# A hybrid DeltaNet, retention and ConvFFN layer: two whole-tile FFN pairs instead of three, and weight splits moved at the v tiles

## What is computed

```python
def mixer_block(hn, pos, w_in, conv_w, a_log, dt_bias, gdn_norm, w_out):
    proj = hn @ w_in                      # q, k, v, z, decay, rotary q and k, retention v, gates
    qkv = silu(causal_dwconv(concat([gq, gk, gv]), conv_w))
    o_a = gated_delta_chunked(gq, gk, gv, log_g, beta)
    o_b = retention_chunked(rq, rk, rv)
    y = sigmoid(gate_a) * y_a + sigmoid(gate_b) * y_b
    return y @ w_out

def conv_ffn(hn, w_up, conv_w, conv_b, w_down):
    u = causal_dwconv(hn @ w_up, conv_w) + conv_b
    a, b = split(u, 2, axis=-1)
    return (silu(a) * b) @ w_down
```

## Time and profile before

| what | before |
|---|---|
| median of 3 runs | 1952.65 us (1951.92 to 1953.54) |
| the profiled execution | 1952.48 us |
| its span, first to last instruction | 1950.7 us |
| PE busy | 1927.2 us, 99% of the span |
| DVE busy | 1283.2 us, 66% |
| ACT busy | 796.1 us, 41% |
| POOL busy | 332.2 us, 17% |
| PE instructions | 13173 matmuls, each with a weight load |

### The profile page before, as it was taken

How to read it: one execution, slowest core, us unless ns; L and a number is a source line. 1 busy time by engine, 2 the same in 40 slices (tenths; PEclk the granted TensorE clock), 3 DMA queues, 4 the chain that set the end, 5 groups by cost and what they waited for, 6 DMA issues and landing times.

```text
span 1950.7 us, 32138 instructions
## 1 busy us (share of the span) xinstructions
PE 1927.2 (99%) x13173; PEld 1859.5 (95%) x13173; DVE 1283.2 (66%) x1612; ACT 796.1 (41%) x1094; POOL 332.2 (17%) x327
## 2 busy tenths in 40 slices
PE   8999999999999999999999999999999999999998
PEld 7999997999999999999999999999999999988887
DVE  6456764747675767677544334389988889877656
ACT  5223432534343444444443333234444344445443
POOL 0000002566574122221101101200000000000001
PEclk9999999999999999999999999999999999999999
DMA  9666566655555575555545552222433555578654
GB/s 296 222 205 141 129 169 191 201 173 161 166 185 141 145 212 162 172 144 157 162 114 157 169 147 87 87 90 60 130 100 109 152 152 162 152 263 277 192 189 159
DMA packets 301222, 315.99 MB, mean 162 GB/s; under 512 B 151004, under 2 KB 221124, under 8 KB 300948
## 3 DMA queue, kind: packets, MB, share of 16 engines
q1 hardware_dynamic: 291860, 290.86, 48.1%
q0 software_dynamic: 9216, 23.07, 5.9%
HBM read 222.76 MB, written 114.18 MB: 173 GB/s over the span
## 4 chain that ended last, share of the span: by engine, by line
PE 92%; DVE 3%; DMA 2%; ACT 1%; issue 1%; POOL 1%; DVEq 0%; SPq 0%; ACTq 0%; POOLq 0%
PE a_psum L1171 35%; PE a_psum L1467 18%; PE a_psum L1477 11%; PE a_psum L155 11%; PE a_psum L1158 5%; PE a_psum L1258 1%; PE a_psum L1277 1%; DMA w_raw<-in_w_in 1%; PE a_psum L1255 1%; PE a_psum L1363 1%; PE a_psum L1287 1%; PE a_psum L1347 1%; PE a_psum L1378 1%; PE a_psum L1303 1%; PE a_psum L1386 1%
## 5 line engine op out<-in xcount | busy, mean ns | idle before, releaser
L1171 PE MATMUL a_psum<-xh,w_hi 128*128 128x342 f32 (+3 forms) x1632 | 528.7, 324 | 3.0 <-DVE w_lo L1936 1.9
L1171 PE MATMUL a_psum<-xl,w_hi 128*128 128x342 f32 (+3 forms) x1632 | 523.1, 321 | 0.0
L1171 PE MATMUL a_psum<-xh,w_lo 128*128 128x342 f32 (+3 forms) x1632 | 521.3, 319 | 0.0
L1171 PEld LDWEIGHTS a_psum<-xh,w_hi 128*128 128x128 f32 x1632 | 307.2, 188 | 6.1 <-DVE w_lo L1936 2.5
L1171 PEld LDWEIGHTS a_psum<-xl,w_hi 128*128 128x128 f32 x1632 | 307.3, 188 | 0.8
L1171 PEld LDWEIGHTS a_psum<-xh,w_lo 128*128 128x128 f32 x1632 | 307.1, 188 | 0.0
L1622 ACT ACTIVATE post<-a_psum 128x342 f32<-128x342 f32 (+3 forms) x204 | 93.2, 457 | 486.0 <-PE a_psum L1171 455.0
L1936 DVE TENSOR_TENSOR w_lo<-w_raw,w_hi 128x1024 fp32r<-128x1024 f32 x86 | 111.1, 1292 | 131.4 <-ACT w_hi L1547 131.3
L1547 ACT ACTIVATE w_hi<-w_raw 128x1024 fp32r<-128x1024 f32 x86 | 90.6, 1053 | 100.8 <-PE a_psum L155 63.0
L1467 PE MATMUL a_psum<-x_t_hi,up_hi 128*128 128x256 f32 x608 | 123.6, 285 | 2.7 <-DVE post L2424 2.5
L1477 PE MATMUL a_psum<-act_hi,down_hi 128*128 128x512 f32 (+1 forms) x324 | 124.4, 384 | 0.0
(11 more groups left out here) (294 smaller groups left out, 3954.9 us busy)
## 6 DMA issues: line engine op xcount, KB each, us to landing
w_raw<-in_w_in SPq DMA_DIRECT2D x75, 512.0 KB, 3.8
up_raw<-in_w_up SPq DMA_DIRECT2D x19, 1024.0 KB, 5.0
mix_scratch<-post SPq DMA_DIRECT2D x32, 522.0 KB, 2.8
down_sums<-in_w_ffn_down POOLq DMA_DIRECT2D x4, 2816.0 KB, 29.4
act_scratch<-post SPq DMA_DIRECT2D x22, 512.0 KB, 2.7
down_raw<-down_sums SPq DMA_DIRECT2D x44, 256.0 KB, 2.7
act_raw<-act_sums SPq DMA_DIRECT2D x44, 256.0 KB, 3.0
ext<-mix_scratch SPq DMA_DIRECT2D x9, 1024.0 KB, 7.6
```

The costliest lines, as they stand in the source:

```text
L1171: mm = pe.matmul(psum[:, u % 2, 0:n], w[:, k, :], x[:, k, at0:at0 + n], start=(k == 0 and part == 0), stop=(k == KC - 1 and part == 2))
```

## The change

`J0` goes from 3 to 2: pair 2 becomes the first Strassen pair, and everything that stood at `J0 - 1` and `J0 - 2` moves one pair earlier. A semaphore `x_free` is incremented by PE when the last whole tile has read blocks 0 to 3 of `xh` and `xl`; the high parts 1 and 3 and the sum `x_t4` wait for it and no longer for the whole tile. DVE's order in between is rewritten. The semaphore that this takes is won by folding `pe_xss` into `rms_ready`.

In `front_plan()`, at the last two v tiles: `dec` and `dec_e` of chunk 0 move from step 91 to step 92, which is behind ACT's copy of third (46, 2); the load of tile 48 moves in front of the stores of tile 44's turned v; and the split of tile 48 moves from behind third (47, 0) to step 92, in front of the turning of v tile 45. (Step u is the third (16 + u // 3, u % 3).)

```diff
-J0 = 3
+J0 = 2
...
-        if j == 0 and not T_RV - 1 <= t < T_Q - 1:
+        if j == 0 and not T_RV - 1 <= t < T_Q - 1 and t != T_ZB - 1:
             add(("split", t + 1))
...
-    steps[91] += [("dl_k", 0), ("expand", 0), ("dec", 0), ("dec_e", 0)]
-    steps[92] += [("qk", 0), ("dl_g", 1), ("dl_m", 1), ("dl_x", 1)]
+    steps[91] += [("dl_k", 0), ("expand", 0)]
+    steps[92] += [("dec", 0), ("dec_e", 0), ("qk", 0), ("dl_g", 1), ("dl_m", 1), ("dl_x", 1)]
...
-        if u == 93:
+        if u in (90, 93):
             weights(t, j)
             add(("vstore", t - 2))
         for step in sorted(steps[u], key=lambda step: step[0] in ("tin", "tout")):
             add(step)
-        if u == 95:
-            add(("split", T_ZB + 1))
+        if u in (92, 95):
+            add(("split", T_ZB + u // 95))
...
-            if u != 92:
+            if u not in (89, 92):
                 add(("vstore" if T_V <= t - 1 else "kstore", t - 1))
-        if t > T_K and u != 93:
+        if t > T_K and u not in (90, 93):
             weights(t, j)
...
                 if ks[-1] == KC - 1:
                     mm.then_inc(units_done, 3)
+                elif t == T_UP + 2 * J0 - 1:
+                    mm.then_inc(x_free, 1)
...
-                    up(j, s, range(KC))
+                    up(j, s, range(KC // 2))
+                    up(j, s, range(KC // 2, KC))
...
             def x_part_high(n):
-                if n not in (0, 2):
+                if n in (1, 3):
+                    act.wait_ge(x_free, 1)
+                elif n > 3:
                     act.wait_ge(units_done, tiles_done(T_UP + 2 * J0 - 1))
...
-                    dve.wait_ge(units_done, tiles_done(T_UP + 2 * J0 - 1))
+                    dve.wait_ge(x_free, 1)
                     dve.wait_ge(x_prep, x_sum_of(1))
...
                 if j == J0 - 1:
                     taps(j, 0)
                     x_part_low(2)
+                    x_part_low(3)
                 evacuate(j, 1)
...
-            x_part_low(3)
             x_sums(3)
             x_part_low(1)
             x_part_low(4)
             x_part_low(5)
+            x_part_low(6)
             combine(0, 0)
             combine(0, 1)
-            x_part_low(6)
             taps(J0 - 1, 1)
             combine(0, 2)
```

More of the change, by code:

```diff
@@ L587, in program @@
         x_in = [sem(f"x_in{n}") for n in range(5)]
-        a_xsq, d_xss, pe_xss, rms_ready, normed, x_hi, x_split = (sem(n) for n in (
-            "a_xsq", "d_xss", "pe_xss", "rms_ready", "normed", "x_hi", "x_split"))
+        a_xsq, d_xss, x_free, rms_ready, normed, x_hi, x_split = (sem(n) for n in (
+            "a_xsq", "d_xss", "x_free", "rms_ready", "normed", "x_hi", "x_split"))
         w_in = [sem(f"w_in{s}") for s in range(3)]
@@ L1164, in _ @@
                     if u in (6, 7):
-                        pe.wait_ge(rms_ready, 3)
+                        pe.wait_ge(rms_ready, 4)
                     else:
@@ L1203, in _ @@
                         mm = pe.matmul(psum[:, bank, at0:at0 + c1 - c0], ones, post[4][:, c0:c1], start=True, stop=True)
-                    mm.then_inc(pe_xss, 1)
+                    mm.then_inc(rms_ready, 1)
                     first_two(1, range(KC // 2, KC))
@@ L1577, in first_two @@
                                        psum[:, 2 + 3 * s:5 + 3 * s, 0:N3], ACT.Copy).then_inc(evac, 3)
-                    act.wait_ge(pe_xss, 1)
+                    act.wait_ge(rms_ready, 1)
                     for bank, at0, c0, c1 in XSS:
@@ L1582, in _ @@
                                        scale=1.0 / D).then_inc(rms_ready, 1)
-                    act.wait_ge(rms_ready, 3)
+                    act.wait_ge(rms_ready, 4)
                     act.activation(rms, rms, ACT.Exp, scale=-0.5).then_inc(rms_ready, 1)
@@ L1994, in _ @@
                         dve.wait_ge(rope_in, 32)
-                        dve.wait_ge(rms_ready, 4)
+                        dve.wait_ge(rms_ready, 5)
                         for n in range(2):
                             dve.tensor_tensor(rope[:, n, :], rope[:, n, :], rms, ALU.mult).then_inc(rms_ready, 1)
-                        dve.wait_ge(rms_ready, 6)
+                        dve.wait_ge(rms_ready, 7)
                     dve.wait_ge(evac, 6 * i + 6)
```

## The result

| what | before | after |
|---|---|---|
| median | 1952.79 us (1951.92 to 1953.54, 4 runs) | 1961.66 us (1960.98 to 1962.89, 4 runs) |
| ratio | | 1.0046, 95% interval 1.0034 to 1.0058 |
| the profiled execution, its span | 1952.48, 1950.7 us | 1962.89, 1961.1 us |

What follows compares the result with a forecast made beforehand. The prediction took PE, 99% busy, as the bound. Profiled 1952.5 us plus 4.8 for the FFN and 4.1 for the v tiles gave 1961.4, rounded up to 1961.5; range 1955.5 to 1964.5 us.

Steps and rivals of the forecast that it cites:

- Part A: FFN, one whole pair replaced by a product pair: 2.50 us less work, but a dearer transition; +4.8 us in all.
- the late evacuation: Transition to Strassen pairs: DVE starts evacuating up(1, 1) only at 1324.8, so PE waits 7.7 us before product 2.
- I take the same here, 1.45: Pair 1 of the FFN: half clock behind the 2.3 us wait before product 5 costs 1.45 us.
- +3.4 without the second fall: Lower case for the FFN part: no clock fall behind the wait before product 5 of pair 1, +3.4 us.
- The transition costs 5.8 now: First two Strassen pairs before the change: 46.20 us against 40.4 without waits, 3.18 of waits and about 1.5 slow clock.
- Part B: Reorders at the last v tiles: two waits vanish, but PE starts (48, 1) 2.6 us later, plus 1.5 half clock; +4.1.
- the price of the clock: V tiles: half clock behind PE's 5.3 us idle before (48, 1) costs 1.5 us.
- the second collision: V tiles: chunk 1's second decay instruction on DVE falls into POOL's pair at 692.18 and ends near 695.3.
- A gain ahead of (48, 1) survives only if DVE's chain is earlier as well: V tiles: ACT's copy of (47, 2) had no slack, so PE's 2.5 us lead needs an earlier DVE chain.
- What POOL holds up: V tiles: tile 48's low part on DVE is held until POOL's read ends at 684.1, done at 685.3; memset holds nothing.
- B is neutral: Rival 1: the low part at the v tiles isn't held, -0.1 us there, FFN loss as computed; 1957.2 us, chance 0.15.
- faster: Rival 2: DVE isn't behind, up(1, 1)'s evacuation starts by 1317.2, v tiles keep a 2.3 gain; 1947.7 us, chance 0.07.

Runs made afterwards that it cites:

- e4: The changed kernel with low part 3 of x moved behind the evacuation of up(1, 1), where it stood before; 1961.01 us, ratio 1.0037.
- e8: The changed kernel with the sum x_t4 computed twice on DVE, to the same values; 1962.85 us, ratio 1.0047.
- e1: The changed kernel without the edits of front_plan(), so the FFN part alone; 1956.85 us, ratio 1.0017.
- e2: The kernel before with only the edits of front_plan() at the v tiles; 1957.27 us, ratio 1.0022.
- e13: e2 with POOL's second multiplication of the qk step cut to 128 of 1024 columns for chunk 0; 1954.30 us, ratio 1.0004.
- e3: The changed kernel with the decay matrix and exponentials of chunk 1 one step later; 1956.76 us, ratio 1.0018.
- e7: e2 with e3's edit and the silu of tile 46 behind unit (47, 2); 1953.11 us, ratio 0.9998.
- e12: Changed FFN with three whole pairs, pair 1's product and sums behind combine(1, 1), the v-tile moves, e3's edit, third (48, 0) before tile 46's silu; 1952.99 us.
- e5: e2 with the split of tile 48 back at its old place behind third (47, 0); 1954.10 us, ratio 1.0006.

## Why the prediction was right, and where it was not

**Part A, the late evacuation: right.** Forecast a wait of 7.7 before product 2, found 7.53; from DVE's evacuation to the end of combine(1, 1) 36.9 us were laid out (1324.8 to 1361.7), found 36.70 (1331.85 to 1368.55). The method, adding up DVE's list and looking for the places where PE meets it, hit to 0.2 us, and e4 and e8 show that it is the list and not one place in it.

**Part A, the size: too large.** Forecast +4.8, found +3.3 in the traces (3.17 and 0.17) and +3.6 by e1's run times. The failed step is one term, "I take the same here, 1.45": half clock behind the wait before product 5 of pair 1. It was taken over from the wait of 2.51. The wait came out at 1.72, not 2.3, and the clock held. PE was ready 35.1 us behind the start of the evacuation instead of 34.8, since the half clock behind product 2 lasted 4.0 us, a loss of 2.0 and not 1.45, and DVE's list ended 0.2 earlier. The case "+3.4 without the second fall" stood beside it and is what happened.

**Part A, the balance of before.** "The transition costs 5.8 now" counted the slow clock behind product 6 as a cost. It wasn't one: the stretch is 106.63 in before with that fall and 106.65 in e2 without it, because DVE's list ends at the same moment and the wait before product 5 is 0.67 in the one and 1.7 in the other. The forecast itself didn't rest on it.

**Part B, the path: right.** The low part held until POOL's read ends (e13), the convolution later by it, the second decay instruction falling into POOL's pair (in after, though not in e2), the copy of (47, 2) at the end: the start of (48, 1) was forecast 2.6 later and came 2.7 later, the wait 5.3 and came 5.36. Run times give +4.0 for B (e2), forecast +4.1. That agrees partly by luck, since the price of the clock was too low and the second collision happens only sometimes. (In e2's trace the second collision is missing: (48, 1) starts only 1.7 later, and the half clock behind it then lasts 5.6 us.) In the profiled execution of after B is +6.6: at the next copy on ACT the lag has grown from 3.13 to 5.42, so the fall cost 2.3 and not 1.5, and 1.6 more were lost near 738. Before, this copy stood at 698.26; after:

```profile
703.68 0.46 ACT L1625 ACTIVATE post<-a_psum 128x342 f32<-128x342 f32 x1 [5.08 <-PE a_psum L1171]
```

**"A gain ahead of (48, 1) survives only if DVE's chain is earlier as well": right,** and stronger than I put it: e3, e7 and e12 make that chain harmless and meet the next one.

**What POOL holds up: right.** The Trainium skill (SBUF — State Buffer, Who interferes with whom) says that a two-input DVE instruction and a GpSimd instruction that reads SBUF exclude each other and that one that only writes is no bar. The trace agrees: in e13 the low part waited for the read of 0.46 and then ran through beside the memset of 0.53. One row was read wrongly. The prediction says that the low part of the earlier trace rows lasted "to the moment when POOL's ended", and once more that it "ended with POOL's read"; it ended at 563.93, 1.07 behind POOL's 562.86. That is a hold until POOL's end and then its own time, which is how the sum counted it (684.1 and then 685.3), so nothing in the forecast changes.

**The rivals.** "B is neutral" is refuted by e2, "faster" by e1 and e4: even with low part 3 out of its way the evacuation comes 5.4 us too late. The first rival's price, -0.1 if the low part isn't held, left out the clock. In e13 the low part is nearly free and (48, 1) starts at 694.19, as in before, but behind a wait of 2.68, and half clock follows: the next copy on ACT is 1.6 later than in before. Against the median of the whole change the two errors, A too large by 1.2 to 1.5 and the small terms of B too small, stand against each other; that 1961.5 met 1961.66 is closer than the steps deserve. Two ends of ranges don't follow from their terms, without bearing on the result: POOL's second operation in front of the decay instruction is half of 3.78 more, so B's high end is +6.0 and not +5.3, and 4.8 with 5.3 gives 1962.6 and not 1963.5.

**What stays open.** Why the clock falls near 736 to 740 in some executions (after, e1, e2, e5) and not in the other ten (in e5 it began at 731). Why it stays at half for 4.0 us in one execution and 6.0 in another behind the same wait. And whether POOL's second collision could be removed without new waits; it wasn't tried.

## What to carry to other kernels

When an engine works through a fixed list and the bound engine meets it at several places, the waits tell where they meet, not what it costs: sum the list up to the last meeting, and expect that moving one item in it moves the wait and gains nothing. Look for that engine's idle times inside the list; they are what an order can win (2.99 us here, all of it), and the cover that a slower variant of the bound engine's work gives may be worth more than the shorter work (2.5 us less work here, and still 6.2 us lost). Before an instruction is moved on DVE, look at what POOL reads at the new time.
